# Softmax inverses sent through DRAM instead of through a transpose on TensorE, in a hybrid attention layer on one core

## The chip, the cores and the metric

The kernel runs on one core of a Trainium2 chip. The metric is the device time of one execution in microseconds (us). The core has five engines with a queue each: TensorE (PE; its weight loads are shown apart as PEld), VectorE (DVE), ScalarE (ACT), GpSimd (POOL) and SyncE (SP), which here only issues transfers. The queues run side by side; each runs its instructions in the order in which they are written, and they wait for each other with semaphores.

## The reference, cut to what matters

Two layers (DEPTH = 2), 1024 tokens, width 1024, float32. In each layer one projection of the normed input gives the queries, keys and values of two attention branches and two sets of gate logits:

```
h = rms_norm(x);  qa, ka, va, qb, kb, vb, gate_logits = split(h @ w_in)
A (8 heads of 64, bias table, 576-key band per 64-token chunk):
    p = softmax(q k^T / 8 + bias);                 y_a = (p v) @ w_branch_a
B (8 heads, 2 key heads, rotary, 128-key window, one learned sink per head):
    m = max(max(s), sink);  p = exp(s - m) / (sum exp(s - m) + exp(sink - m)); y_b = (p v) @ w_branch_b
x = x + (g_a * y_a + g_b * y_b) @ w_out;   x = x + SwiGLU(rms_norm(x))
```

The kernel does not divide p by its sum before the product with v. It multiplies the 64 output features of a head by 1 / sum afterwards, per token. The output is stored with features on the partitions and tokens along the row, while the sums stand with tokens on the partitions; so the inverses have to be turned, and each repeated over the 64 partitions of its head.

## The kernel before, in words

Each layer has four stretches: the input projection, attention, the branch and output projections, and the feed-forward part. Only attention is touched; in the trace its scores run from 281 to 527 us in layer 0 and from 1613 to 1860 us in layer 1.

Attention runs over UNITS = 128 **units**. A unit is one head of one 128-query block in branch A, or one chunk of 64 tokens (two heads of it side by side) in branch B. Units go by groups (GROUPS = 4) of 32: a phase of 16 A units (PHASE = 16), then a phase of 16 B units. Two units that follow each other (e = 0 and 1) make one pair, and a pair has one output tile of 128x128. Every engine has its own loop over **slots** `s`, written out by hand; there is no scheduler. In slot s:

- PE (`attention`, L1501 to 1527) computes the scores of unit s (L1412, L1413), one step of the gate projection (`gate_step`; three 512-column matmuls, L1266, L1270, L1271), turns the softmax rows of unit s-2 (`turn`, L1424), and in even slots turns the inverses of unit pair s-5 (`turn_wide`, L1464), multiplies the pair s-3 with the values (`weigh`, L1452), and takes the other gate steps. At some slots it turns a part of v (`turn_values`, L1387). `turn_wide` writes in the same PSUM bank as `turn_values`: so it waits for ACT's copies of the values (`v_ready`), and `turn_values` waits for `head_scaled`.
- DVE takes the maximum of the scores plus bias (`row_max`, L2691), and in odd slots multiplies a pair's outputs by the turned inverses (`scale_heads`, L2719), in even slots computes the inverses of a pair (`invert_pair`, L2708 and L2710; L2697 for the sinks). The rest is splitting queries, keys and rotary operands (L2639, L2648, L2651, L2662 to 2671) and the gate logits (L2732).
- ACT copies a pair's outputs from PSUM to `x_sb` (`take_heads`, L1857), copies the turned rows (`take_turned`, L1846) and the values (`take_values`, L1815), and takes the exponential with the row sum (`soften`, L1825; L1829 for the sinks).
- POOL repeats each pair of inverses over 64 columns (`repeat_inverse`, L1246, into `wide`), and between these splits the weight tiles of the gate projection in high and low halves (`split_part`, L1228, L1231).
- SP loads q, k, v parts (L988, L993, L950), bias rows (L1113), rotary tables (L1094) and weight tiles (L896), and saves gate logits (L1003); it issues one after the other, each after its own waits.

The gate steps are filler work for PE. How many stand in a slot is a table, `fill_rate` (L229): `FILL_A` for A phases (one row for group 0, one for the others), `FILL_B` steps spread evenly over the B phases.

After the last unit PE has the last gate tile to do (`last_gates`, L1482), while ACT and DVE split the scaled outputs (`split_o`, L1882) for the branch projections.

## Time and profile before

| | |
|---|---|
| median of 3 runs | 2699.23 us (2695.42 to 2701.89) |
| profiled execution | 2699.5 us, of which the span from first to last instruction 2697.5 us |
| TensorE granted clock, mean | 0.994 |
| PE busy | 2633.4 us (98%) |
| DVE busy | 1919.6 us (71%) |
| ACT busy | 1155.7 us (43%) |
| POOL busy | 296.0 us (11%) |

PE is the busiest engine over the whole span, but its share counts a matmul up to its modelled end; inside attention there are gaps. A row of the timeline or of the waits names the idle time before an instruction and what ended it ("<-DVE stat L2691"). PE and PEld are two rows of one engine: a wait can be booked on the weight load (PEld), while a former matmul still runs on PE.

### The profile page before, as it was taken

Reading aid. Unit: us, or ns where it says so; the run is one execution under the profiler, and the core shown is the slowest. Engines: PE = TensorE matmul, PEld = TensorE weight load, DVE = VectorE, ACT = ScalarE, POOL = GpSimd, SP = SyncE. Lnnn points to the kernel's source line nnn. Section 1 sums busy time; section 2 is a strip of 40 time slices with the busy share of each in tenths; the row PEclk is TensorE's granted clock in tenths of the full one; section 3 lists DMA queues with packets and bytes.
Section 4 is the critical chain, followed back from the end, with each engine's and each line's share of the span. In section 5 each row is a group of like instructions: output and inputs, shape, how many; then the busy total and the mean of one; then the engine's idle time right before and its main releaser. Section 6 shows DMA issues by size and latency. Waiting matters only on the chain. (4 is left out here: it accounts for less than half of the span.)

```text
span 2697.5 us, 36792 instructions
## 1 busy us (share of the span) xinstructions
PE 2633.4 (98%) x12920; PEld 2146.6 (80%) x12920; DVE 1919.6 (71%) x3579; ACT 1155.7 (43%) x2365; POOL 296.0 (11%) x518
## 2 busy tenths in 40 slices
PE   8999999999999999999999999999999999999998
PEld 6888767788888888888878886677888888888887
DVE  8766666654787777768996666666447887776687
ACT  6222677632533333344542227776325333333444
POOL 0000212244200000000000012223440000000000
PEclk9999999999999999999999999999999999999999
DMA  4323433253223332386423243332531322334843
GB/s 150 121 102 118 149 98 103 73 174 123 94 94 106 113 108 88 109 266 177 151 102 117 105 147 110 111 96 80 194 125 50 127 98 92 107 114 128 269 127 125
DMA packets 185397, 333.22 MB, mean 124 GB/s; under 512 B 17280, under 2 KB 62976, under 8 KB 185216
## 3 DMA queue, kind: packets, MB, share of 16 engines
q1 hardware_dynamic: 176992, 307.67, 34.7%
q10 hardware_dynamic: 8224, 23.20, 2.5%
q8 instruction: 105, 1.72, 0.3%
q14 instruction: 76, 0.62, 0.1%
HBM read 237.09 MB, written 92.80 MB: 122 GB/s over the span
## 5 line engine op out<-in xcount | busy, mean ns | idle before, releaser
L1278 PE MATMUL ps<-op_hi,up_hi 128*128 128x512 f32 x1232 | 479.9, 390 | 2.5 <-DVE third_sum L2871 2.5
L1280 PE MATMUL ps<-op_hi,up_lo 128*128 128x512 f32 x1232 | 479.3, 389 | 0.0
L1279 PE MATMUL ps<-op_lo,up_hi 128*128 128x512 f32 x1232 | 479.3, 389 | 0.0
L1278 PE MATMUL ps<-in_hi,up_hi 128*128 128x512 f32 x728 | 286.6, 394 | 2.4 <-DVE up_lo L2367 2.1
L1280 PE MATMUL ps<-in_hi,up_lo 128*128 128x512 f32 x728 | 285.2, 392 | 0.0
L1279 PE MATMUL ps<-in_lo,up_hi 128*128 128x512 f32 x728 | 285.2, 392 | 0.0
L1966 ACT ACTIVATE up_hi<-up_raw 128x512 fp32r<-128x512 f32 x252 | 158.0, 630 | 278.6 <-PE ps L1280 271.4
L1278 PEld LDWEIGHTS ps<-op_hi,up_hi 128*128 128x128 f32 x1232 | 231.2, 188 | 51.2 <-issue 3.3
L1280 PEld LDWEIGHTS ps<-op_hi,up_lo 128*128 128x128 f32 x1232 | 231.2, 188 | 48.1
L1279 PEld LDWEIGHTS ps<-op_lo,up_hi 128*128 128x128 f32 x1232 | 231.2, 188 | 47.9
L1278 PE MATMUL ps<-act_hi,dn_hi 128*128 128x512 f32 x616 | 240.3, 390 | 1.2 <-DVE dn_lo L3046 1.2
L1279 PE MATMUL ps<-act_lo,dn_hi 128*128 128x512 f32 x616 | 239.7, 389 | 0.0
L1280 PE MATMUL ps<-act_hi,dn_lo 128*128 128x512 f32 x616 | 239.6, 389 | 0.0
L1228 POOL CAST w_hi<-w_raw 128x256 fp32r<-128x256 f32 x192 | 83.2, 474 | 1370.1 <-DMA w_raw<-w_lin 1190.0
L1676 ACT ACTIVATE up_hi<-w_quarter 128x512 fp32r<-128x512 f32 x156 | 96.7, 628 | 193.1 <-PE ps L1280 180.4
L2838 DVE TENSOR_TENSOR up_lo<-up_raw,up_hi 128x512 fp32r<-128x512 f32 x252 | 172.4, 686 | 0.0
L1993 ACT ACTIVATE act_hi<-act_raw 128x512 fp32r<-128x512 f32 x154 | 97.0, 630 | 173.8 <-DMA act_raw<-ff_saved 170.9
L1231 POOL TENSOR_TENSOR w_lo<-w_raw,w_hi 128x256 fp32r<-128x256 f32 x192 | 164.4, 885 | 0.0
L1278 PEld LDWEIGHTS ps<-in_hi,up_hi 128*128 128x128 f32 x728 | 138.1, 190 | 32.3 <-DVE up_lo L2367 3.2
L3044 DVE TENSOR_TENSOR act_lo<-act_raw,act_hi 128x512 fp32r<-128x512 f32 x154 | 106.2, 689 | 80.0 <-ACT act_hi L1993 79.6
L1279 PEld LDWEIGHTS ps<-in_lo,up_hi 128*128 128x128 f32 x728 | 137.9, 189 | 28.6
L1280 PEld LDWEIGHTS ps<-in_hi,up_lo 128*128 128x128 f32 x728 | 137.8, 189 | 28.6
(266 smaller groups left out, 5270.0 us busy)
## 6 DMA issues: line engine op xcount, KB each, us to landing
up_raw<-w_gu SPq DMA_DIRECT2D x42, 1024.0 KB, 5.1
act_raw<-ff_saved SPq DMA_DIRECT2D x154, 256.0 KB, 2.7
w_quarter<-w_lin SPq DMA_DIRECT2D x52, 512.0 KB, 4.5
w_raw<-w_lin SPq DMA_DIRECT2D x48, 512.0 KB, 3.6
ff_saved<-ff_block SPq DMA_DIRECT2D x88, 256.0 KB, 2.0
ff_saved<-ff_mix SPq DMA_DIRECT2D x66, 256.0 KB, 2.1
gated<-gates_saved SPq DMA_DIRECT2D x32, 512.0 KB, 4.2
stage<-in_saved SPq DMA_DIRECT2D x48, 256.0 KB, 2.8
```

Source lines behind the costliest of these rows:

```text
L1228: pool.tensor_copy(w_hi[slot][:, k, :], w_raw[raw][:, k, :]).then_inc(hi_made, 1)
L1231: op = pool.tensor_tensor(w_lo[slot][:, k, :], w_raw[raw][:, k, :], w_hi[slot][:, k, :], ALU.subtract)
L1278: pe.matmul(out, w1, x1, start=first, stop=False, skip_group_check=True)
L1279: pe.matmul(out, w1, x0, start=False, stop=False, skip_group_check=True)
L1280: return pe.matmul(out, w0, x1, start=False, stop=last, skip_group_check=True)
L1676: act.activation(up_hi[s % PRODUCTS][:, :, :], in_weight(q, i), ACT.Copy).then_inc(in_raised, 1)
L1966: act.activation(up_hi[s % PRODUCTS][:, :, :], up_src(q, i), ACT.Copy).then_inc(up_raised, 1)
L1993: act.activation(act_hi[r][:, :], act_raw[r][:, :], ACT.Copy).then_inc(act_raised, 1)
L2838: dve.tensor_tensor(up_lo[s % PRODUCTS][:, :, :], up_src(q, i), up_hi[s % PRODUCTS][:, :, :], ALU.subtract).then_inc(up_split, 1)
L3044: dve.tensor_tensor(act_lo[r][:, :], act_raw[r][:, :], act_hi[r][:, :], ALU.subtract)
```

## The change: what it does

- The outputs of a pair are copied from PSUM to `x_sb` by DVE (`take_heads`) one slot earlier in its order than the scaling was, in ACT's place; ACT's copy is gone.
- Maxima, sums, sink terms and inverses stand in four arrays of 16 columns. The inverses of four units (a **quarter**, QUARTER = 4) are computed by one reciprocal of 128x4; the sink terms likewise.
- SP stores the 128x4 inverses turned to a DRAM buffer of 4x128 (`save_inverse`: 512 runs of 4 bytes) and loads them back, each row repeated over 64 partitions, with two transfers into `inverse_rows` (`spread_inverse`). DVE scales four units by one multiply of 128x256 (`scale_heads`). In a quarter that begins at unit 4q the inverse is made at DVE's slot 4q+4 (A) or 4q+5 (B), saved in SP's slot 4q+6, spread in its slot 4q+8, and used in DVE's slot 4q+11.
- `turn_wide` on PE and `repeat_inverse` on POOL are gone, with the two waits that the shared bank asked for. POOL splits the weight tiles as soon as they can be, not in portions by slot.
- The gate steps: `FILL_A`'s second row begins with a step, `FILL_B` rounds up instead of down, and in the first slot of each phase a gate step stands ahead of the scores.
- After attention ACT waits for the last save before its first `o_hi`, and for the last scaling only before `o_hi` 6.

```diff
-NSTAT = 8
+NSTAT = 16
+QUARTER = 4
-FILL_A = ((3, 3, 3, 3, 2, 3, 1, 2, 1, 1, 0, 1, 1, 1, 0, 1), (0, 1, 0, 2, 0, 1, 0, 1, 0, 1, 0, 1, 0, 1, 0, 0))
+FILL_A = ((3, 3, 3, 3, 2, 3, 1, 2, 1, 1, 0, 1, 1, 1, 0, 1), (1, 1, 0, 1, 0, 1, 0, 1, 0, 1, 0, 1, 0, 1, 0, 0))
...
-    return FILL_B[g] * (r + 1) // PHASE - FILL_B[g] * r // PHASE
+    return (FILL_B[g] * (r + 1) + PHASE - 1) // PHASE - (FILL_B[g] * r + PHASE - 1) // PHASE
...
+SAVED_AT, SPREAD_AT, SCALED_AT = 6, 8, 11
...
+            def save_inverse(L, quarter):
+                n = L * QUARTERS + quarter
+                sp.wait_ge(inverse_ready, n + 1)
+                sp.dma_start(inverse_dram[n].rearrange("u n -> n u"), inverse[:, stats_of(quarter)],
+                             allow_slow_non_contiguous=True).then_inc(inverse_saved, 16)
+            def spread_inverse(L, quarter):
+                n = L * QUARTERS + quarter
+                sp.wait_ge(inverse_saved, 16 * (n + 1))
+                if n > 0:
+                    sp.wait_ge(head_scaled, n)
+                for e in range(2):
+                    src = inverse_dram[n].rearrange("(p e) n -> e p n", e=2)[e:e + 1].to_broadcast([HD, 2, P])
+                    sp.dma_start(inverse_rows[e * HD:(e + 1) * HD, :].rearrange("d (p n) -> d p n", p=2), src).then_inc(inverse_spread, 16)
...
-                for s in range(UNITS + 3):
+                for s in range(UNITS + SPREAD_AT):
+                    if s >= SAVED_AT and (s - SAVED_AT) % QUARTER == 0 and s - SAVED_AT < UNITS:
+                        save_inverse(L, (s - SAVED_AT) // QUARTER)
+                    if s >= SPREAD_AT and (s - SPREAD_AT) % QUARTER == 0:
+                        spread_inverse(L, (s - SPREAD_AT) // QUARTER)
...
-                for s in range(UNITS + 2):
-                    if s >= 3 and s % 2 == 1:
-                        repeat_inverse(L, s - 2)
-                    for t, part in split_parts(s):
-                        split_part(L, t, part)
-                for t in range(GATE_TILES, TILES):
+                for t in range(TILES):
                     split(L, t)
...
-                for s in range(UNITS + 5):
+                for s in range(UNITS + 3):
+                    steps = fill_steps(s)
+                    if s % PHASE == 0 and s > 0:
+                        for i, k in steps[:1]:
+                            gate_step(L, i, k)
...
-                    if s >= 6 and s % 2 == 0:
-                        turn_wide(L, s, s - 5)
...
-                        if s >= 6:
-                            pe.wait_ge(head_scaled, L * HEAD_PAIRS + (s - 4) // 2)
                         turn_values(L, c, part)
...
-                    if s >= 5 and s % 2 == 1:
-                        take_heads(L, s - 4)
...
+            def invert(L, quarter):
+                cols = stats_of(quarter)
+                total = row_sum[:, cols]
+                dve.wait_ge(softened, L * UNITS + QUARTER * (quarter + 1))
...
+                dve.reciprocal(inverse[:, cols], total).then_inc(inverse_ready, 1)
+            def take_heads(L, u):
...
+                dve.wait_ge(head_done, n + 1)
+                src = o_ps(u) if mixer == "A" else o_ps(u).rearrange("p (h n) -> p h n", h=2)
+                dve.tensor_copy(x_of(u), src).then_inc(head_free, 1)
+            def scale_heads(L, quarter):
...
+                dve.wait_ge(head_free, L * HEAD_PAIRS + 2 * quarter + 2)
+                dve.wait_ge(inverse_spread, 32 * (n + 1))
+                if mixer == "A":
+                    x = x_sb[:, g, p * P:(p + 2) * P]
+                    dve.tensor_tensor(x, x, inverse_rows[:, :], ALU.mult).then_inc(head_scaled, 1)
```

PE's queue where branch B of group 1 begins (unit 48). `ka_hi` and `kb_hi` are the keys of A and B (scores), `probs` the softmax rows being turned, `wide` the repeated inverses, `va` the values, `w_hi` a gate weight tile. Before:

```order
L1413 MATMUL ps<-ka_lo_94,qs_88 128x384
L1424 MATMUL ps<-ident,probs_107 128x128 x5
L1412 MATMUL ps<-kb_hi_95,qb_first 128x128
L1413 MATMUL ps<-kb_lo_97,qb_first 128x128
L1424 MATMUL ps<-ident,probs_108 128x128 x5
L1464 MATMUL ps<-ident,wide 128x128
L1452 MATMUL ps<-probs_t_112,va 64x128
```

And in the changed kernel, at the same place:

```order
L1419 MATMUL ps<-ka_lo_94,qs_88 128x384
L1430 MATMUL ps<-ident,probs_107 128x128 x5
L1272 MATMUL ps<-in_hi_52,w_hi_230 128x512
L1276 MATMUL ps<-in_lo_59,w_hi_230 128x512
L1277 MATMUL ps<-in_hi_52,w_lo_232 128x512
L1418 MATMUL ps<-kb_hi_95,qb_first 128x128
L1419 MATMUL ps<-kb_lo_97,qb_first 128x128
L1430 MATMUL ps<-ident,probs_108 128x128 x5
L1458 MATMUL ps<-probs_t_112,va 64x128
```

The three matmuls of a gate step stand between the last A rows and the first B scores, and the turn of `wide` ahead of the product with the values is gone.

DVE's queue in the same B phase. The first instruction of each pair on `probs` is `row_max`; `ka_lo` is a key half of the next A phase. Before:

```order
L2691 ISA probs_107,stat<-ps,b_zeros,less_sinks 128x128
L2691 ISA stat 128x1
L2708 TENSOR_TENSOR stat<-stat 128x2
L2710 RECIPROCAL stat<-stat 128x2
L2691 ISA probs_108,stat<-ps,b_zeros,less_sinks 128x128
L2691 ISA stat 128x1
L2697 TENSOR_TENSOR stat<-sink_rows,stat 128x2
L2719 TENSOR_TENSOR x_sb<-ps,x_sb 128x2x64
```

And in the changed kernel, over one quarter:

```order
L2717 COPY x_sb<-ps 128x2x64
L2703 TENSOR_TENSOR sink_term<-row_sum,sink_term 128x4
L2705 RECIPROCAL inverse<-sink_term 128x4
L2744 TENSOR_TENSOR logit_118<-ps,rstd 128x512
L2682 ISA probs_108,neg_max<-ps,b_zeros,less_sinks 128x128
L2682 ISA neg_max 128x1
L2682 ISA probs_109,neg_max<-ps,b_zeros,less_sinks 128x128
L2682 ISA neg_max 128x1
L2717 COPY x_sb<-ps 128x2x64
L2731 TENSOR_TENSOR x_sb<-x_sb,inverse_rows 128x2x128
```

Four small instructions per pair became four per quarter, each pair has a copy, and every second pair also the scaling multiply, which waits for a transfer and has the next `row_max` behind it.

SP's queue from the last loads of group 1's B phase into the A phase behind it (`stage` and `swapped` take operands, `w_raw` the gate weight tile). Before:

```order
L988 DMA stage_103<-in_saved 64x512 x2
L896 DMA w_raw_225<-w_lin 128x1024
L993 DMA stage_104<-in_saved 128x512
L993 DMA stage_103<-in_saved 128x512
L950 DMA swapped<-in_saved 32x512 x4
```

And in the changed kernel:

```order
L903 DMA w_raw_228<-w_lin 128x1024
L1118 DMA inverses_saved<-inverse 128x4x1
L995 DMA stage_103<-in_saved 64x512 x2
L1129 DMA inverse_rows<-inverses_saved 64x2x128 x2
L1000 DMA stage_104<-in_saved 128x512
L1118 DMA inverses_saved<-inverse 128x4x1
L1000 DMA stage_103<-in_saved 128x512
L957 DMA swapped<-in_saved 32x512 x4
```

Between the loads of the operands there is now, per quarter, one save and two spreads, and the spread stops SP until the save has landed.

## Rows read from the trace of the kernel before

**Rows 1.** The page: busy time by engine.
```profile
PE 2633.4 (98%) x12920; PEld 2146.6 (80%) x12920; DVE 1919.6 (71%) x3579; ACT 1155.7 (43%) x2365; POOL 296.0 (11%) x518
```

**Rows 2.** Busy time of stretches: start:end, length, PE PEld DVE ACT POOL, PEclk.
```profile
280.00:532.00 252.00, 234.08 (x1660) 177.51 (x1659) 158.67 (x547) 176.22 (x527) 58.21 (x124) 0.99 0.32 99
337.00:344.00 7.00, 6.43 (x31) 4.54 (x31) 3.41 (x15) 5.66 (x17) 0.59 (x2) 0.76 0.31 81
```

**Rows 3.** PE's and PEld's waits, 280 to 532 us: total, times, longest.
```profile
PE ps L1464 <- ACT vb L1815: 3.8, 4, 2.0
PE ps L1464 <- ACT va L1815: 2.9, 5, 1.4
PE ps L1412 <- DVE qb_second L2648: 1.5, 1, 1.5
PE ps L1464 <- POOL wide L1246: 1.2, 1, 1.2
...
PEld ps L1464 <- issue: 14.0, 22, 2.4
...
PEld ps L1387 <- DVE x_sb L2719: 5.0, 15, 0.6
```

**Rows 4.** Timeline of PE at 305 and 306 us: start, length, instruction.
```profile
305.27 0.27 PE L1424 MATMUL ps<-ident,probs 128*128 128x128 f32 x1
...
306.55 0.71 PE L1424 MATMUL ps<-ident,probs 128*128 128x128 f32 x5
```

**Rows 5.** Timeline of PE in the last B phase, layer 1.
```profile
1851.45 0.44 PE L1452 MATMUL ps<-probs_t,vb 128*64 128x128 f32 x4
...
1852.09 0.45 PE L1266 MATMUL ps<-in_hi,w_hi 128*128 128x512 f32 x1
...
1852.84 0.38 PE L1424 MATMUL ps<-ident,probs 128*128 128x128 f32 x2
...
1853.30 0.30 PE L1464 MATMUL ps<-ident,wide 128*128 128x128 f32 x1
1853.69 0.44 PE L1452 MATMUL ps<-probs_t,vb_odd 128*64 128x128 f32 x4
...
1856.43 0.44 PE L1452 MATMUL ps<-probs_t,vb 128*64 128x128 f32 x4
```

**Rows 6.** Groups of instructions, 280 to 532 us: busy, mean ns, idle before.
```profile
L2719 DVE TENSOR_TENSOR x_sb<-ps,x_sb 128x128 f32<-128x128 f32 x64 | 18.4, 288 | 1.0 <-PE ps L1464 1.0
L2710 DVE RECIPROCAL stat<-stat 128x2 f32<-128x2 f32 x64 | 10.6, 166 | 1.5 <-DVE stat L2708 0.2
L2732 DVE TENSOR_TENSOR logit<-ps,rstd 128x512 f32<-128x512 f32 x14 | 9.6, 688 | 0.1
```

**Rows 7.** Waits of DVE, 280 to 532 us.
```profile
DVE probs L2691 <- PE ps L1413: 53.3, 63, 2.2
...
DVE stat L2708 <- ACT stat L1829: 6.1, 16, 1.0
```

**Rows 8.** Transfers, 280 to 532 us: KB each, median us from issue to landing.
```profile
gates_saved<-logit SPq DMA_DIRECT2D x14, 256.0 KB, 2.1
...
swapped<-in_saved SPq DMA_DIRECT2D x28, 64.0 KB, 2.3
```

**Rows 9.** The same view of the whole execution.
```profile
sinks<-sink_in SPq DMA_DIRECT2D x1, 8.0 KB, 9.7
```

**Rows 10.** SP's own timeline: start, time in which it issues.
```profile
376.51 0.34 SPq L993 DMA_DIRECT2D stage<-in_saved  x1
378.95 0.58 SPq L1094 DMA_DIRECT2D rope<-rope_in  x1
...
397.45 1.09 SPq L988 DMA_DIRECT2D stage<-in_saved  x2
```

**Rows 11.** Timeline at the end of attention in layer 0.
```profile
527.79 0.38 ACT L1846 ACTIVATE probs_t<-ps 128x256 f32<-128x256 f32 x1
...
529.18 0.44 PE L1452 MATMUL ps<-probs_t,vb 128*64 128x128 f32 x4
```

More of the change, by code:

```diff
@@ L585, in x_of, with stat_of, stats_of @@
             return x_sb[:, tile:tile + 2, chunk * CHUNK:(chunk + 1) * CHUNK]
+        def stat_of(u):
+            return slice(u % NSTAT, u % NSTAT + 1)
+        def stats_of(quarter):
+            first = QUARTER * quarter % NSTAT
+            return slice(first, first + QUARTER)
         def turned_to(u):
@@ L1228, in split_part @@
                     pool.tensor_copy(w_hi[slot][:, k, :], w_raw[raw][:, k, :]).then_inc(hi_made, 1)
-                else:
-                    pool.wait_ge(hi_made, W_PARTS * number + first + 1)
+                for part in range(W_PARTS):
+                    k = slice(part * KT // W_PARTS, (part + 1) * KT // W_PARTS)
+                    pool.wait_ge(hi_made, W_PARTS * number + part + 1)
                     op = pool.tensor_tensor(w_lo[slot][:, k, :], w_raw[raw][:, k, :], w_hi[slot][:, k, :], ALU.subtract)
-                    if first == W_PARTS - 1:
-                        op.then_inc(tile_ready, 1)
@@ L1870, in attention @@
                         soften(L, s)
+                    if s >= QUARTER and s % QUARTER == 0 and unit(s - 1)[0] == "B":
+                        soften_sinks(L, s // QUARTER - 1)
                     for e in range(2):
@@ L2712, in scale_heads, with add_sinks @@
-            def scale_heads(L, u):
+                                         ALU.add, ALU.min, neg_max[:, stat_of(u)]).then_inc(scores_free, 1)
+            def add_sinks(L, quarter):
+                _, g, _, _ = unit(QUARTER * quarter)
+                cols = stats_of(quarter)
+                both = sink_rows[:, :].rearrange("p (a h) -> p h a", h=2)[:, g // 2:g // 2 + 1, 2 * L:2 * L + 2]
+                dve.wait_ge(scores_free, L * UNITS + QUARTER * (quarter + 1) + 1)
+                dve.tensor_tensor(sink_term[:, cols].rearrange("p (c e) -> p c e", e=2), both.to_broadcast([P, 2, 2]),
+                                  neg_max[:, cols].rearrange("p (c e) -> p c e", e=2), ALU.add).then_inc(sink_step, 1)
@@ new lines, in scale_heads @@
+            def scale_heads(L, quarter):
+                mixer, g, _, p = unit(QUARTER * quarter)
+                n = L * QUARTERS + quarter
+                dve.wait_ge(head_free, L * HEAD_PAIRS + 2 * quarter + 2)
[3 more added lines that the diff above has]
+                    dve.tensor_tensor(x, x, inverse_rows[:, :], ALU.mult).then_inc(head_scaled, 1)
+                else:
+                    tile, chunk = GROUPS + g // 2 * 2, chunk_of(g, p)
+                    x = x_sb[:, tile:tile + 2, chunk * CHUNK:(chunk + 2) * CHUNK].rearrange("p h (c n) -> p h c n", c=2)
+                    dve.tensor_tensor(x, x, inverse_rows[:, :].rearrange("p (c h n) -> p h c n", c=2, h=2), ALU.mult).then_inc(head_scaled, 1)
@@ L2734, in attention @@
             def attention(L):
-                for s in range(UNITS + 6):
+                for s in range(UNITS + SCALED_AT):
                     if s < UNITS:
                         row_max(L, s)
-                    if s % 2 == 1 and s >= 7:
-                        scale_heads(L, s - 6)
-                    if s % 2 == 0 and 1 <= s <= UNITS:
-                        invert_pair(L, s - 1)
+                    if s % 2 == 1 and 5 <= s < UNITS + 4:
+                        take_heads(L, s - 4)
+                    for late in range(2):
+                        quarter, first = divmod(s - QUARTER - late, QUARTER)
+                        if first == 0 and 0 <= quarter < QUARTERS:
+                            sunken = unit(QUARTER * quarter)[0] == "B"
+                            if late == 0 and sunken:
+                                add_sinks(L, quarter)
+                            if late == (1 if sunken else 0):
+                                invert(L, quarter)
+                    if s >= SCALED_AT and (s - SCALED_AT) % QUARTER == 0:
+                        scale_heads(L, (s - SCALED_AT) // QUARTER)
                     for e in range(2):
```

138 lines of the change are left out of this document (51 added, 87 removed).

## The prediction

> **What bounds the kernel now.** The page comes first: PE is busy for 2633.4 of 2697.5 us [rows 1], so a change can only pay where PE has work less or stands still. Then the stretches: the attention part of layer 0, 280 to 532 us, has 234.1 us of PE busy in 252.0, DVE 158.7 and ACT 176.2 [rows 2]; layer 1 repeats it. So some 18 us per layer are open idle time, and more is hidden, since a matmul counts up to its modelled end. The waits of that stretch tell where: PE's row for the turn of `wide` (L1464) waits 3.8 + 2.9 us for ACT's copies of the values and 1.2 us for POOL, and its weight load stands for 14.0 us more with no releaser named; the transposes of the values wait 5.0 us for DVE's scaling [rows 3]. Last the waits of DVE: it waits 53.3 us for PE's scores [rows 7]. So in attention no single engine is full. PE, DVE and ACT hand units round in a ring, PE has the least slack, and its largest stops are at the very instruction that the change removes.
>
> **What the change removes from PE.** 64 transposes per layer (one per output pair, as many as L2719 has [rows 6]), 128 in all. Five transposes in a row take 0.71 us, one 0.27 [rows 4]: (0.71 - 0.27) / 4 = 0.11 us for each further one, 128 x 0.11 = 14.1 us. Not every one is on the path. At 1853 us the turn of `wide` starts 0.39 us before the product with the values, more than the transpose takes: the product waits for ACT's copy in any case [rows 5]. That is so in roughly a quarter of the pairs, so I take 0.75 x 14.1 = 10.6 us; ends 0 and 14.1.
>
> **The waits at the turn of `wide`.** Booked on PE: 3.8 + 2.9 + 1.2 = 7.9 us per layer; with the weight load's 14.0 it is 21.9, but a wait booked there runs partly beside an older matmul [rows 3]. For two layers the ends are 15.8 and 43.8 us; I take 24, nearer the row in which PE itself is idle. With the instruction the wait goes, and next to be late are the copies of the turned rows (`probs_t`) and the maxima. ACT's queue is in the same order as before, minus one copy per pair, so PE runs ahead of it by a step, and then meets it. I let 60% stay as gain: 14.4 us; ends 0 and 24. The wait at the end of attention (POOL, 1.2 us) is among them: the last product starts 1.39 us after ACT began the last copy of 0.38 us [rows 11], and the changed queue has nothing between.
>
> **The waits at the turns of the values.** They waited for `head_scaled`, 5.0 us per layer on the weight load [rows 3], 10 in all, partly beside older work: 6 as the size, 60% of it stays, 3.6 us; ends 0 and 10.
>
> **The gate step ahead of a phase.** It costs nothing in sum, since the number of steps is the same, and it fills a hole: at unit 48 PE waits 1.5 us for `qb_second` [rows 3]. From the first matmul of a step to what follows it are 1852.84 - 1852.09 = 0.75 us [rows 5]. One such hole per layer, 2 x 0.7 = 1.4 us; ends 0 and 3.0. The new fill table moves steps by a slot or less; I cost it at nothing, since a step hides the copy of `probs_t` wherever it stands between turn and product, and the skipped ones now fall into odd slots, ahead of a turn instead of behind it.
>
> **The clock.** Between 337 and 344 us the granted clock is 0.76 of full speed, so a part of that stretch runs at 1.2 instead of 2.4 GHz; before it PE had stood for 2.0 us, the longest of the waits for ACT's `vb` copy [rows 2, 3]. 7.0 x 0.24 = 1.7 us per layer; if the wait shrinks the fall may go. I take 2 us for both layers; ends 0 and 3.4.
>
> **What it moves to DVE.** Removed per layer: 64 multiplies of 0.288, 64 reciprocals of 0.166 and 64 sink additions that I price like a reciprocal: 18.4 + 10.6 + 10.6 = 39.6 us. Added: 64 copies from PSUM, for which the trace has no row; the multiply of the same size from PSUM takes 0.288, the reciprocal of two columns 0.166, these are my ends and I take 0.288: 18.4. Further 32 multiplies of 256 columns: 128 columns take 0.288, 512 take 0.688 [rows 6], so 0.288 + 128 x (0.688 - 0.288) / 384 = 0.42, 13.4 us; 32 reciprocals and 32 sink additions, 10.6. Together 42.4, or 2.8 us more of 158.7: no new bound by itself. But order matters: in every second odd slot the copy and the multiply, 0.71 us instead of 0.29, now stand ahead of the next maximum. If all of that were on the path it would be 64 x 0.42 = 27 us; DVE waits 53.3 us per layer for scores [rows 7], so most of it is covered: 3 us. The wait of DVE for ACT's sink exponentials, 6.1 us per layer [rows 7], goes since the sum is now read a slot later; on PE's path I credit 1 us for both layers, ends 0 and 12.
>
> **What it adds on SP, and the wait behind it.** The multiply waits for `inverse_spread`, and behind it on DVE stands the next `row_max`, for which PE waits. In a B phase there are six slots from the reciprocal to the multiply. Four slots take 1856.43 - 1851.45 = 4.98 us in the last group, which has 12 gate steps in 16 slots [rows 5]; that is 1.25 each, in the other groups (14 steps) 0.75 x 2 / 16 = 0.09 more, 1.34. Without the transpose (0.11 per two slots) they are 1.19 and 1.28, six of them 7.1 and 7.7, less 0.33 for sum and reciprocal: 6.8 and 7.4 us. Against that stands the chain. A store of 128 runs lands in 2.1 us [rows 8]. SP issues 128 runs in 0.34 us and 256 in 0.58 [rows 10], so 512 in 1.06, 0.72 more: 2.8 us, and I take 3.2 for the writes of 4 bytes; ends 2.1 and 9.7, the latter the slowest small transfer of the trace, queued behind large ones [rows 9]. Then two spreads: the second is issued 0.55 us after the first (half of 1.09 [rows 10]) and lands 2.3 us later, as a 64 KB load does [rows 8]: 2.85. In sum 6.1, with semaphores 6.2: inside 6.8 and 7.4, though narrowly. SP itself is held 3.2 + 1.1 = 4.3 us of a quarter of 4.8 to 5.1, and the operand loads between (1.09 us for two) can make it late by half a microsecond. I take 0.5 us in 8 of the 32 B quarters: 4 us; low end 0, high end below. In A phases a unit has up to five times as many columns and there are seven slots, so nothing is late.
>
> The Trainium skill ("DMA: Bandwidth & Descriptors", section Specifications) says that transfers with runs below 512 bytes make the DMA engine read, modify and write. The trace of before has no store with runs that short, so no run here shows it; it is a reason for the third rival below, and if it made the save cost twice my value it would be that case.
>
> **The sum.** Gains 10.6 + 14.4 + 3.6 + 1.4 + 2 + 1 = 33.0, losses 3 + 4 = 7, net 26 us. The profiled execution took 2699.5 us, within 0.3 us of the median of the runs (2699.23), so the forecast is 2673.5, rounded 2673 us.
>
> **Rivals.**
> - *The waits only move.* PE meets ACT and DVE a step later and waits there. For it: ACT and DVE already sit at 70% and 63% of the stretch [rows 2], and ACT's late copies of the values come from ACT's own backlog. Against it: DVE waits longer for PE than PE for DVE. Then remain the transposes, a fifth of the 24 us and the clock, 10.6 + 4.8 + 2 - 7 = 10: 2689 us.
> - *DVE's heavier slots are on the path.* The 27 us are paid instead of 3: 33 - 27 - 4 = 2, so 2698 us. Against it speak the same 53.3 us.
> - *The save is slow, and B phases run at the pace of the transfers* (slower than before). Each quarter's multiply then waits, the next maximum with it, and six slots last as long as the chain. With a save of x us a slot is (x + 2.95 + 0.33) / 6, against a mean of 1.26; over 128 B slots it eats all gains of 30 us from an excess of 0.24 on, a slot of 1.50, x = 5.7 us. At x = 6.5 it is 1.63, 0.37 x 128 = 47 us lost, 33 - 47: about 2714 us. At the end of 9.7 us it would be 2.16 per slot, 115 us lost, some 2780. For it: 512 runs of 4 bytes, and SP standing still behind them. Against it: all stores of the stretch land in about 2 us.
>
> **Chances.** Forecast 0.50, waits that move 0.22, DVE on the path 0.13, slow save 0.15. The likeliest case alone reaches from 2658 (most of the waits gone) to 2684. For the whole I give 2655 to 2703: 0.06 lies below, 0.13 above, almost all of it the slow save. A difference of 0.2% (5.4 us) is about what a measurement of this kernel can tell from none. Faster by more: 0.49 of the first case, 0.19 of the second, 0.04 of the third, 0.01 of the last, 0.73. Within: 0.01 + 0.02 + 0.06 + 0.01 = 0.10. Slower: the rest, 0.01 + 0.03 + 0.13 = 0.17.
>
> **What would show it.** Right: no idle above 0.5 us before the product with the values in group 0 of A, the stretch from the first score to the first matmul of the last gate tile shorter by about 13 us in each layer, and nothing changed behind it, since PE's last gate tile covers the later start of `o_hi`. The save's row should have 2.8 to 3.6 us to landing, the spread's 2.3 to 2.6, and DVE's multiply little idle time before it. Wrong: a row in which that multiply waits for the transfer in most B quarters, with PE's B scores waiting for the maxima behind it (slow save); PE waits for `probs_t` or the maxima grown by what L1464 has lost (moved waits); or ACT waiting for `stage` loads that SP issued late, a case which I hold small, since a half-microsecond of lateness is less than the room between a load and its use.

## The result, and the profile after

The changed kernel takes 2980.5 us (median of 4 runs, 2968.41 to 2982.84), against 2697.32 us (4 runs) for the kernel before on the same chip: ratio 1.1038, 95% interval 1.1004 to 1.1072. It is 283 us slower, where 26 us faster was forecast. The profiled execution has a span of 2980.9 us and a mean granted clock of 0.938, against 0.994.

The page, then the stretch of attention in layer 0, cut at 656 us, 5 us after its last scores (before at 532; the scores ended at 525); the third line is the B phase of group 1 (columns as in [rows 2]):

```profile
PE 2695.8 (90%) x12792; PEld 2182.7 (73%) x12792; DVE 1914.1 (64%) x3515; ACT 1127.9 (38%) x2205; POOL 244.9 (8%) x390
```

```profile
280.00:656.00 376.00, 258.83 (x1581) 192.71 (x1579) 154.67 (x503) 160.18 (x442) 31.64 (x55) 0.77 0.41 73
...
422.30:474.10 51.80, 30.44 (x167) 21.85 (x168) 14.59 (x61) 14.61 (x49) 4.20 (x8) 0.70 0.36 53
```

PE, 98% busy in [rows 1], is at 90%. The stretch is 376 us long instead of 252 [rows 2]. PE's busy time in it rose from 234 to 259 us for less work: the granted clock fell from 0.99 to 0.77, so close to half of the stretch ran at 1.2 instead of 2.4 GHz, each time after PE had stood (2.0 to 5.3 us in one piece). The other 99 of the 124 us are idle time. Layer 1 lost as much: from its first to its last scores there are 372.4 us, before 243.9. DVE, ACT and POOL do less than before and became no bound.

The waits of PE, DVE, ACT and SP in that stretch, as in [rows 3, 7]:

```profile
PE ps L1458 <- ACT probs_t L1844: 39.6, 8, 9.2
PE ps L1418 <- DVE neg_max L2682: 28.8, 13, 6.1
PE ps L1393 <- DMA stage<-in_saved: 18.0, 4, 9.0
```

```profile
DVE probs L2682 <- PE ps L1419: 51.6, 38, 10.0
...
DVE x_sb L2727 <- DMA inverse_rows<-inverses_saved: 33.2, 8, 8.6
DVE ka_lo L2631 <- ACT ka_hi L1776: 30.9, 11, 7.4
DVE x_sb L2731 <- DMA inverse_rows<-inverses_saved: 24.8, 8, 7.2
```

```profile
ACT ka_hi L1776 <- DMA stage<-in_saved: 63.8, 10, 11.6
...
ACT qs L1774 <- DMA stage<-in_saved: 17.2, 4, 8.3
```

```profile
SPq L1129 <- DMA inverses_saved<-inverse: 170.4, 30, 9.1
SPq L1126 <- DVE x_sb L2727: 31.8, 12, 6.0
```

Two kinds of late data stand here side by side. DVE waits 58 us for the spread inverses (L2727 is the multiply of an A quarter, L2731 of a B quarter). But ACT waits 81 us for `stage`, a load of q or k that has nothing to do with the inverses, and DVE's `ka_lo` waits for ACT behind it. Before, ACT's wait for `stage` was 0.3 us:

```profile
ACT ka_hi L1780 <- DMA stage<-in_saved: 0.3, 1, 0.3
```

The transfers say the same. `stage` before (280 to 532 us), then three rows of now [rows 8]:

```profile
stage<-in_saved SPq DMA_DIRECT2D x21, 256.0 KB, 2.8
```

```profile
stage<-in_saved SPq DMA_DIRECT2D x21, 256.0 KB, 8.6
inverse_rows<-inverses_saved SPq DMA_DIRECT2D x60, 64.0 KB, 3.6
...
gates_saved<-logit SPq DMA_DIRECT2D x13, 256.0 KB, 9.4
```

The store of the gate logits landed in 2.1 us and now takes 9.4. One quarter shows the chain, in the timelines of SP, DVE, ACT and PE:

```profile
333.20 0.46 SPq L1118 DMA_DIRECT2D inverses_saved<-inverse  x1
333.79 2.41 SPq L1137 DMA_DIRECT2D rel_sb<-rel  x4
343.52 1.26 SPq L1129 DMA_DIRECT2D inverse_rows<-inverses_saved  x2
344.88 2.11 SPq L995 DMA_DIRECT2D stage<-in_saved  x2
```

```profile
348.13 0.42 DVE L2727 TENSOR_TENSOR x_sb<-x_sb,inverse_rows 128x256 f32<-128x256 f32 x1 [7.12 <-DMA inverse_rows<-inverses_saved]
```

```profile
349.04 0.63 ACT L1776 ACTIVATE ka_hi<-stage 128x512 fp32r<-128x512 f32 x1 [8.57 <-DMA stage<-in_saved]
...
350.87 0.36 ACT L1844 ACTIVATE probs_t<-ps 128x256 f32<-128x256 f32 x1
```

```profile
351.33 0.69 PE L1458 MATMUL ps<-probs_t,vb_odd 128*64 128x128 f32 x4 [9.79 <-issue]
```

From the save's issue to the spread's issue pass 10.3 us; over all 64 quarters it is 7.6 to 12.0, median 9.4. SP issues the four `rel_sb` loads in it and then stands, from 336.2 to 343.5 us, so the `stage` loads behind it are issued only at 344.88. DVE's multiply waits 7.1 us with the maxima behind it. But what ends last ahead of PE is on ACT: it stands 8.6 us for `stage`, and the copy of the turned rows (`probs_t`) that PE's product reads stands behind that. PE's row names no releaser; its 9.8 us end 0.1 us after that copy. So in this quarter SP's standing reached PE by the late load; the multiply had been done since 348.55.

### The profile page after: what moved, and what is told of

It is laid out like the page before. It is cut to its first block and busy times, and to the rows that moved or that the text cites. A ratio compares the mean times of both kernels' runs of the same rounds, so it can differ in the third digit from the quotient of the medians.

```text
span 2980.9 us, 36091 instructions
## 1 busy us (share of the span) xinstructions
PE 2695.8 (90%) x12792; PEld 2182.7 (73%) x12792; DVE 1914.1 (64%) x3515; ACT 1127.9 (38%) x2205; POOL 244.9 (8%) x390
## 5 line engine op out<-in xcount | busy, mean ns | idle before, releaser
L1820 ACT ACTIVATE probs<-probs,neg_max 128x128 f32<-128x128 f32 (+5 forms) x256 | 138.7, 542 | 96.6 <-DVE neg_max L2682 95.1
```

What stands on the lines that cost most here:

```text
L1820: act.activation(buf[:, c0:c1], buf[:, c0:c1], ACT.Exp, bias=neg_max[:, stat_of(u)], scale=-1.0, accum_out=row_sum[:, stat_of(u)]).then_in ...
```

## The experiments

**First set: the whole loss, and where it sits.** Its expectations number the theories; 1 is that the transfers of the inverses are the whole loss.

`no_transfer` leaves out save and spreads; DVE multiplies by a constant.

```diff
-                        save_inverse(L, (s - SAVED_AT) // QUARTER)
-                        spread_inverse(L, (s - SPREAD_AT) // QUARTER)
+                        pass
...
+            pool.memset(inverse_rows[:, :], 0.01).then_inc(consts_made, 1)
```

> The changed kernel without save and spreads: SP issues neither, DVE multiplies by a constant buffer instead of the inverses, and nothing waits for a transfer (the output is therefore not scaled by the true inverses). All the rest of the change stays: DVE's copies, the multiply of 128x256 per four units, no turn of wide on PE, the moved gate steps. Theory 1 (the transfers are the whole loss, whether by the wait of DVE or by what they do to other transfers): 2660 to 2685 us, the 2673 us of the forecast less its 4 us for the spread. Theory 2 (DVE's heavier odd slots, the copy and the multiply ahead of the next maximum, carry a part of the loss): above 2700 us, up to 2900.

Measured: 2660.9 us, ratio to before 0.9862 (0.9846 to 0.9878). The transfers are the whole loss; all the rest of the change gains 37.5 us. From the first to the last scores of a layer there are 226.3 us, against 244.1 before (they end near 525 us, not 527 as the text ahead of the prediction has it) and 370.7 in the changed kernel. The stretch from 281 to 513 us, columns as in [rows 2]:

```profile
281.00:513.00 232.00, 218.75 (x1596) 166.76 (x1595) 157.41 (x514) 161.00 (x446) 34.40 (x60) 1.00 0.35 106
```

Almost the same matmuls (1596 against 1581 recorded) keep PE busy for 219 us here and for 259 in the changed kernel. So of the loss some 40 us per layer, 80 of 320 us, are busy time that goes with the lower clock; the rest is time in which PE stands.

`late_use` keeps the 4-byte saves, but spreads and uses the inverses much later:

```diff
-SAVED_AT, SPREAD_AT, SCALED_AT = 6, 8, 11
+SAVED_AT, SPREAD_AT, SCALED_AT = 6, 16, 19
```

> The changed kernel with the spread at SP slot 4q+16 instead of 4q+8 and the multiply at DVE slot 4q+19 instead of 4q+11: ten slots between save and spread, so that nobody stands still for the save to land. The same transfers are issued. Theory 1a (the loss is the wait: DVE's multiply and SP stand for the chain of save and spread): 2670 to 2700 us. Theory 1b (the save holds the DMA queues, so that the operand loads and gate logits behind it land late, whoever waits for the save itself): still above 2800 us, with landings of 8 us for the operand loads and ACT and DVE waiting for stage.

Measured: 2897.1 us, ratio 1.0733 (1.0703 to 1.0763). Room for the save gives back 83 of 283 us. How much of the loss is the wait for the save can't be read from this alone: SP now stands 103 us between 280 and 680 us for the multiply of the quarter before, more than the 50 us of the changed kernel. `save_only` below shows the part that needs no such wait.

`flat_save` stores the same 2 KB as 128 runs of 16 bytes, a token's four inverses in each:

```diff
-                sp.dma_start(inverse_dram[n].rearrange("u n -> n u"), inverse[:, stats_of(quarter)],
-                             allow_slow_non_contiguous=True).then_inc(inverse_saved, 16)
+                sp.dma_start(inverse_dram[n].rearrange("u (r c) -> (u r) c", c=QUARTER), inverse[:, stats_of(quarter)]).then_inc(inverse_saved, 16)
```

> The changed kernel, where the save writes the inverses as they stand, 128 runs of 16 bytes into one 2 KB block, instead of turned (512 runs of 4 bytes with 512 bytes between neighbours of a partition); the spread then reads the block in another order, so the outputs are scaled by inverses of other tokens. Bytes, waits and places are those of the changed kernel. Theory 1c (the cost is in the number of short runs): the save needs a quarter of its time, 3 to 4 us instead of about 9, and the kernel takes 2680 to 2730 us. Theory 1d (any store to DRAM followed by a load back under a standing SP costs this): 2900 us or more.

Measured: 2689.9 us, ratio 0.9954 (0.9937 to 0.9971). Its transfers between 280 and 520 us:

```profile
stage<-in_saved SPq DMA_DIRECT2D x22, 256.0 KB, 3.5
inverse_rows<-inverses_saved SPq DMA_DIRECT2D x61, 64.0 KB, 2.7
...
gates_saved<-logit SPq DMA_DIRECT2D x13, 256.0 KB, 3.8
...
inverses_saved<-inverse SPq DMA_DIRECT2D x31, 2.0 KB, 3.1
```

The save lands in 3.1 us and the other transfers nearly as before. It is the form of the save that costs. I took the number of its runs for the cause; that fell later.

`gates_only` is the kernel before, with nothing but the new fill table and the gate step ahead of a phase's first scores:

```diff
+                    if s % PHASE == 0 and s > 0:
+                        for i, k in steps[:1]:
+                            gate_step(L, i, k)
...
```

> The kernel before with the gate steps alone changed: the new fill table and the gate step ahead of a phase's first scores. The forecast credited 1.4 us of gain, ends 0 and 3: 2696 to 2698 us. If the skipped steps in odd slots let the copies of probs_t stand bare between turn and product less often, up to 5 us more; if the moved steps take cover away elsewhere, up to 5 us slower.

Measured, in 5 runs: 2688.5 us, ratio 0.9962 (0.995 to 0.9975), a gain of 10 us, more than any reading had. In the profiled runs 1.8 us of it lie ahead of the first scores (279.2 against 281.0 us), where the edit changes nothing, so in that pair of runs it is 8.

**Second set: the save alone, and a save in another form.**

`save_only` is `no_transfer` with the 32 saves of each layer put back on SP; nobody reads them. (The texts on record for `save_only` and `rows_saved` say 16 saves and 16 transposes; it is 32 of each in a layer.) Two completion counters take turns, so SP waits for the save before the last, and DVE for one four quarters back before it overwrites the inverses; between 280 and 680 us no wait ended on either. `save_only_act` has the saves on ACT's own queue.

```diff
+                if n >= 2:
+                    sp.wait_ge(saved_of[n % 2], 16 * ((n - 2) // 2 + 1))
                 sp.wait_ge(inverse_ready, n + 1)
...
```

> The changed kernel without its spreads, but with its 16 saves of the inverses (512 runs of 4 bytes each) issued on SyncE's queue where the changed kernel issues them; VectorE multiplies by a constant and nobody uses what was saved (the scaling of the outputs is left out). SyncE stands only for the save before the last. The kernel without any of these transfers took 2661 us. Theory Q (a save holds up the transfers issued behind it, and engines wait for their late loads): stage loads land in 7 to 9 us in attention instead of 2.8, and the time is 2780 to 2890 us. Rival W (what costs is the chain save, spread, multiply, release of a bank): nothing waits for the save here, so 2655 to 2675 us. The kernel with late users (2897 us) speaks for Q, since spacing the chain gave back only 83 of 283 us.

> As the kernel with saves alone, but ScalarE issues them on its own DMA queue, at the same place in the row of units (scaling left out likewise). If what is held is SyncE's queue (each of its descriptors waits its turn behind the save's), SyncE's loads land in about 3 us again and the time is 2661 to 2690 us. If what is held is the DMA engines or the memory that the save writes to, whatever queue it stands on, stage loads land in 7 to 9 us again and the time is that of the kernel with saves alone within 20 us. I hold the second likelier, 3 to 2, as the spreads of the changed kernel too landed late without standing directly behind a save.

Measured: 2799.9 us on SP (1.0381, 1.0365 to 1.0397) and 2840.7 us on ACT (1.0539, 1.0524 to 1.0553). Transfers between 280 and 520 us, on SP first:

```profile
stage<-in_saved SPq DMA_DIRECT2D x19, 256.0 KB, 8.2
...
gates_saved<-logit SPq DMA_DIRECT2D x11, 256.0 KB, 8.7
```

```profile
stage<-in_saved SPq DMA_DIRECT2D x18, 256.0 KB, 10.8
...
gates_saved<-logit SPq DMA_DIRECT2D x10, 256.0 KB, 9.7
...
inverses_saved<-inverse ACTq DMA_DIRECT2D x21, 2.0 KB
```

A save that nobody waits for costs 139 us: ACT waits 42.4 us for `stage` before `ka_hi` (280 to 680 us), before 0.3. And SP's loads are late too when the save stands on another queue: what is held up is not SP's queue but something behind both, the DMA engines or the memory. The dearer case was the one on ACT, by 41 us, outside the 20 us that I had allowed; why, no run tells.

`rows_saved` turns the inverses on the chip: one transpose of PE per quarter, in the spare half of the output bank, a copy by DVE, and a save of 4 runs of 512 bytes.

```diff
-SAVED_AT, SPREAD_AT, SCALED_AT = 6, 8, 11
+SAVED_AT, SPREAD_AT, SCALED_AT = 8, 11, 15
...
-                sp.dma_start(inverse_dram[n].rearrange("u n -> n u"), inverse[:, stats_of(quarter)],
-                             allow_slow_non_contiguous=True).then_inc(inverse_saved, 16)
+                sp.dma_start(inverse_dram[n], inverse_turned[:, :]).then_inc(inverse_saved, 16)
...
+                    pe.transpose(turned_ps(u), inverse[:, stats_of(quarter)], ident[:, :])
...
+                    dve.tensor_copy(inverse_turned[:, :], turned_ps(u))
```

> The changed kernel with the inverses turned on the chip first: TensorE transposes the quarter's 128x4 inverses once for four units (16 transposes in all), VectorE copies the 4x128 result, and SyncE saves 4 runs of 512 bytes instead of 512 runs of 4; the save is issued in slot 8 of a quarter instead of 6, the spread in 11, the first use in 15. By theory Q the save then lands in 2 to 3 us, stage loads in about 3 us, and the time is near that of the kernel without the transfers (2661 us) plus 16 copies of about 0.3 us and some waiting: 2662 to 2682 us. If the spreads (two of 128 partitions each) are a cost of their own, 2685 to 2700 us, as the kernel with a flat save (2690 us) would then have shown for the same reason.

Measured: 2691.5 us (11 runs), ratio 0.9981 (0.9973 to 0.999). The loads land in about 3 us, but the time missed its 2662 to 2682. It falls in the range of the other reading, a cost of the spreads themselves; the third set shows another reason.

`flat_late` is the flat save with slots 6, 10, 15, and the spread ahead of the save where both fall in one slot:

> The kernel with the flat save (128 runs of 16 bytes; the outputs are scaled by other tokens' inverses), with the spread issued in slot 10 and ahead of the next save, and the first use in slot 15, so that SyncE and VectorE hardly wait for a transfer. The flat save took 2690 us, 29 us over the kernel without transfers. If those 29 us are the waits of SyncE and VectorE for save and spread: 2664 to 2678 us. If they are other loads held for a while by the 16-byte runs: 2682 to 2692 us, no change.

Measured: 2785.8 us, ratio 1.0331 (1.0317 to 1.0346), 96 us worse than `flat_save`, which neither reading had. SP between 280 and 680 us:

```profile
SPq L1125 <- DVE x_sb L2730: 71.6, 15, 9.1
SPq L1125 <- DVE x_sb L2726: 69.2, 13, 8.7
```

There is one buffer `inverse_rows`. With 10 and 15 the spread of a quarter (slot 4q+10) stands in SP's order ahead of the slot in which DVE makes the multiply of the quarter before (4q+11), and SP waits 141 us for it, with every load behind it (57 us in `flat_save`). The room between spread and use must stay under four slots.

**Third set: the slots.** The three kernels with rows saved differ in one line each, and `late_gap` is `late_use` with 6, 14, 16:

```diff
-SAVED_AT, SPREAD_AT, SCALED_AT = 8, 11, 15
+SAVED_AT, SPREAD_AT, SCALED_AT = 8, 11, 14
```

> As the kernel with the inverses turned on TensorE and saved as rows (2691.5 us), with save, spread and first use in slots 8, 11, 14 instead of 8, 11, 15. There is one buffer for the spread inverses, so the spread of a quarter waits for the multiply of the quarter before, which comes 4 slots before this quarter's own. With 8, 11, 15 both fall in one slot, and SyncE stood 94 us at that wait between 280 and 680 us, with the loads behind it. Now one slot lies between them. If this standing is what the 30 us over the kernel without transfers are: 2672 to 2684 us. If they are the added transposes, copies and issues (32 of each): 2688 to 2694 us.

> As rows_a with 8, 12, 15: the same one slot between the multiply before and the spread, but the save has 4 slots to land before SyncE waits for it. It lands in 2 to 3 us, and two slots of a B phase are 3 us, so the fourth slot should give nothing: within 4 us of rows_a. Should it be over 5 us faster, SyncE stood for the save, not for the multiply.

> As rows_a with 8, 12, 14: two slots between the multiply before and the spread, and two from the spread to its use. SyncE's standing for the multiply should be nearly gone, but VectorE has 3 us in a B phase for a transfer of 2.6 us behind 1.2 us of issues, and may now wait for it, 1 us in each of 16 B quarters. If SyncE's standing decides: 2665 to 2680 us, faster than rows_a by 3 or more; if VectorE's wait decides: slower than rows_a.

> The kernel with 4-byte saves and late users, with save, spread and use in slots 6, 14, 16 instead of 6, 16, 19. The version with 6, 16, 19 took 2897 us, 97 us more than the saves alone without any spread (2800 us), and SyncE stood 103 us between 280 and 680 us for the multiply of the quarter before. Theory S (beside the held transfers, worth 139 us, the rest is SyncE standing at its waits with the loads behind it): two slots of room instead of one take a third to two thirds of the standing away, 2830 to 2870 us. Rival: the rest is what the spreads' own transfers lose behind a save; then it stays at 2885 to 2905 us, or becomes slower, as the users wait 2 slots after the spread instead of 3.

| kernel | slots | us | ratio to before (95%) |
|---|---|---|---|
| rows_a | 8, 11, 14 | 2668.2 | 0.9887 (0.9872 to 0.9902) |
| rows_b | 8, 12, 15 | 2677.9 | 0.9923 (0.9908 to 0.9938) |
| rows_c | 8, 12, 14 | 2682.0 | 0.9937 (0.9923 to 0.9952) |
| late_gap | 6, 14, 16 | 2930.9 | 1.0857 (1.0835 to 1.0879) |

`rows_a` beats both kernels, by 30 us the one before. Nothing of the change is left out in it; it is 7 us over `no_transfer`, with 32 transposes and copies per layer as added work. Its rows, the waits between 280 and 680 us and the groups between 280 and 520:

```profile
SPq L1131 <- DVE x_sb L2741: 35.8, 15, 6.5
SPq L1131 <- DVE x_sb L2745: 21.2, 10, 3.9
```

```profile
L2729 DVE COPY inverse_turned<-ps 4x128 f32<-4x128 f32 x32 | 8.8, 274 | 0.1
L1463 PE MATMUL ps<-ident,inverse 128*4 128x128 f32 x32 | 8.7, 272 | 2.7 <-ACT probs_t L1853 1.5 <-DVE inverse L2714 1.2
```

One slot less between spread and use gave 23 us. `rows_b` missed its forecast (10 us slower than `rows_a`, not within 4), and `rows_c` went the way of its second branch, though DVE waits for the spread only 16.3 us in it, against 7.0 in `rows_a`, so that wait alone doesn't explain its 14 us. A spread in slot 12 stands behind the next quarter's save, which is issued in the same slot and waits for DVE's copy; that order moved SP's standing from the multiply to that copy (63.5 us in `rows_b`, 14.9 in `rows_a`). `late_gap` did not give theory S what it forecast: SP's standing for the multiply fell from 103 to 29 us, and yet the time rose by 34. But it doesn't refute the theory, for its slot 14 has the order of `rows_b`: the spread stands behind a later quarter's save, and at that save SP now stands 122 us for DVE's inverses (21 in `late_use`). SP's standing only changed its place, and DVE's wait for the spread grew:

```profile
SPq L1118 <- DVE inverse L2705: 122.4, 27, 9.8
```

```profile
DVE x_sb L2727 <- DMA inverse_rows<-inverses_saved: 74.6, 15, 9.0
DVE x_sb L2731 <- DMA inverse_rows<-inverses_saved: 61.6, 13, 8.6
```

In `late_use` these two were 28.9 and 25.3. In the slots tried here, with a save of 4-byte runs, moving spread and use changed who waits, not whether.

**Fourth set: what in the save is slow.** All five are `save_only` with its save changed: a quarter of the runs, or all 512 moved apart in DRAM.

```diff
-        inverse_dram = nc.dram_tensor("inverses_saved", (DEPTH * QUARTERS, QUARTER, P), F32, kind="Internal").ap()
+        inverse_dram = nc.dram_tensor("inverses_saved", (DEPTH * QUARTERS, QUARTER, P, 16), F32, kind="Internal").ap()
...
-                sp.dma_start(inverse_dram[n].rearrange("u n -> n u"), inverse[:, stats_of(quarter)],
+                sp.dma_start(inverse_dram[n][:, :, 0].rearrange("u n -> n u"), inverse[:, stats_of(quarter)],
...
```

> The kernel with the saves alone (2800 us, 139 over the kernel without transfers), with a quarter of each save: the inverses of one of the four units, 128 runs of 4 bytes (the scaling is left out). If the price goes by the count of runs: stage loads land in 3.3 to 4.5 us and the time is 2665 to 2695 us, like the 128 runs of 16 bytes. If a 4-byte run costs more than a 16-byte one whatever their number, or a save has a fixed price: over 2720 us.

> The saves alone, 512 runs of 4 bytes as before, but every run is written 64 bytes apart in DRAM instead of right behind its neighbour (the scaling is left out). If the runs are slow because neighbours, written by different DMA engines, fall into one small block of DRAM and wait for each other: stage loads near 3 us, 2661 to 2700 us. If it is the count of small writes: as the saves alone, 2785 to 2815 us. I hold the second likelier, 2 to 1.

> As save_spaced, with the runs 512 bytes apart, for blocks larger than 64 bytes (the scaling is left out). Neighbours waiting for each other: 2661 to 2700 us here, and more at 64 bytes where the block is larger than that. Count of small writes: 2785 to 2815 us, the same as at 64 bytes and as side by side.

> As save_spaced (4-byte runs 64 bytes apart, 2664 us), but 16 bytes apart, so that 4 runs share 64 bytes of DRAM instead of 1, or of 16 side by side (2800 us); the scaling is left out. The flat save, with four 16-byte runs to 64 bytes, landed in 3.1 us. If the price goes by how many writes fall into one block of 64 bytes: 4 of 16, so 139 us x 4/16 = 35 us over 2661: 2680 to 2715 us. If the block in which writes wait for each other is 16 bytes or smaller: 2661 to 2670 us. If only the count mattered, 2800 us, which the spaced saves already speak against.

> The same with the runs 32 bytes apart: 2 share 64 bytes (the scaling is left out). A block of 64 bytes: 139 us x 2/16 = 17 us, so 2665 to 2690 us, between the ones at 16 and at 64 bytes. A block of 32 bytes or smaller: as at 64 bytes, 2661 to 2668 us.

| 4-byte runs of a save | from one to the next | us (2 runs each; save_only and no_transfer 4) | `stage` lands in |
|---|---|---|---|
| 512 (save_only) | 4 bytes | 2799.9 | 8.2 us |
| 128 (save_quarter) | 4 bytes | 2761.8 | 7.6 us |
| 512 | 16 bytes | 2668.0 | 3.4 us |
| 512 | 32 bytes | 2665.4 | 3.0 us |
| 512 | 64 bytes | 2663.8 | 2.7 us |
| 512 | 512 bytes | 2661.5 | 3.0 us |
| none (no_transfer) | | 2660.9 | 2.8 us |

The row that kills my theory of the count is that of the 128 runs of 4 bytes, between 280 and 520 us:

```profile
stage<-in_saved SPq DMA_DIRECT2D x21, 256.0 KB, 7.6
...
inverses_saved<-inverse SPq DMA_DIRECT2D x25, 0.5 KB, 9.3
```

A quarter of the runs lands as late as all of them (9.4 us to the next issue in the changed kernel), and costs 101 of the 139 us. And 512 runs of 4 bytes cost 3 us in the whole kernel once they start 64 bytes apart, which these few runs can't tell from nothing: the ratio to before is 0.9882 (0.9853 to 0.9911), that of `no_transfer` 0.9862 (0.9846 to 0.9878). Size and count are the same there; only the neighbourhood differs. The loss comes from 4-byte writes directly beside each other. The 16-byte runs of `flat_save` also lie side by side, and cost little: four of them fill 64 bytes, as four of the 4-byte runs do at 16 bytes from one to the next. That distance suffices for nearly all of it (8 bytes was not tried), at the edge of what I had expected for a small block (2661 to 2670 us). I had held this the less likely reading, 1 to 2.

**Last, the changed kernel itself with only the addresses changed:**

```diff
-        inverse_dram = nc.dram_tensor("inverses_saved", (DEPTH * QUARTERS, QUARTER, P), F32, kind="Internal").ap()
+        inverse_dram = nc.dram_tensor("inverses_saved", (DEPTH * QUARTERS, QUARTER, P, 16), F32, kind="Internal").ap()
...
-                    src = inverse_dram[n].rearrange("(p e) n -> e p n", e=2)[e:e + 1].to_broadcast([HD, 2, P])
+                    src = rope_in[4 * (n % 8):4 * (n % 8) + 4, 0, 0:P].rearrange("(p e) n -> e p n", e=2)[e:e + 1].to_broadcast([HD, 2, P])
```

> The changed kernel (2980.5 us) with everything in its place, the save of 512 runs of 4 bytes in slot 6, the spread in slot 8, the multiply in slot 11, and all the waits, but with the 4-byte runs written 64 bytes apart. So that the spread still reads rows of 512 bytes, it takes them from an input instead (the outputs are scaled by numbers of the rotary table, not by the inverses). Theory N (neighbouring 4-byte writes in one block are the whole loss): the save lands in 2 to 4 us, stage loads in about 3.5 us, and the time is that of the kernel with the flat save, 2690 us, within 12 us. Rival: with the chain of save, spread and multiply behind it, 512 small writes cost something wherever they go: 2720 us or more.

Measured: 2725.7 us, ratio 1.0103 (1.0086 to 1.012). The edit takes 255 of the 283 us away, with the save, the spreads and all waits in place. But it misses theory N's 2690 us by 36: the rival's bound of 2720 is passed. Its rows between 280 and 680 us, transfers and then DVE:

```profile
stage<-in_saved SPq DMA_DIRECT2D x21, 256.0 KB, 4.4
...
inverse_rows<-rope_in SPq DMA_DIRECT2D x64, 64.0 KB, 4.3
```

```profile
DVE x_sb L2731 <- DMA inverse_rows<-rope_in: 18.7, 7, 7.2
```

In `flat_save` these are 3.5, 2.7 and 7.8 us, and its save lands in 3.1 us against 4.2 here. So 512 separate writes still delay what shares the path where someone waits for them, or the other source of the spread does; the run changed both and can't tell these apart.

## Why the prediction was wrong

- **What bounds the kernel: right.** PE has the least slack: without the transfers it is busy for 219 of 232 us in attention, DVE for 157 and ACT for 161.
- **The gains: near in sum, in part by luck.** Forecast 33.0 less 3 for DVE's order, 30; measured 37.5 without the transfers. On the kernel before, the gate step with its table gave 10 (8 of them in the part that it touches), forecast 1.4 with ends 0 and 3: mis-sized. I had priced one hole at unit 48; the edit also changes the fill table, which I costed at nothing, and which of the two brings it no run tells. If it gives as much in the changed kernel, the remaining 27 us stand against 28.6 forecast for transposes, waits, clock and sinks less DVE's order; how they split was not tried.
- **DVE: its prices were right.** The copy from PSUM takes 286 ns, forecast 288; the reciprocal of four columns 178, forecast 166; the multiply of 256 columns 420 in A as forecast, 476 in B. DVE's wait for scores did not become smaller (51.6 against 53.3) in a stretch half as long again, and in `no_transfer` nothing stands behind DVE that cost the gain.

```profile
L2717 DVE COPY x_sb<-ps 128x128 f32<-128x128 f32 x62 | 17.7, 286 | 0.0
L2727 DVE TENSOR_TENSOR x_sb<-x_sb,inverse_rows 128x256 f32<-128x256 f32 x16 | 6.7, 420 | 33.2 <-DMA inverse_rows<-inverses_saved 33.2
L2731 DVE TENSOR_TENSOR x_sb<-x_sb,inverse_rows 128x256 f32<-128x256 f32 x13 | 6.2, 476 | 24.8 <-DMA inverse_rows<-inverses_saved 24.8
```

- **SP's issue: wrong on the safe side.** 512 runs were to take 1.06 us; the timeline has 0.46 at 333.20 us and 0.59 at 349.60.
- **The save's price: the step that failed.** "I take 3.2 for the writes of 4 bytes; ends 2.1 and 9.7." It is 7.6 to 12.0 us until the spread is issued, near and over the upper end. SP's waits in between end on the save 30 times (170 us) and on DVE's multiply 20 times (46 us), so most of it is the save. The choice went by the nearest rows, stores of 2048-byte runs, when the one property that differed, 4-byte runs side by side, was the one that mattered. The Trainium skill ("DMA: Bandwidth & Descriptors", section Specifications) has runs under 512 bytes read, modified and written. That warned in the right direction, but it goes by size alone, and by it the runs 16 bytes apart (4 bytes each) should cost as much as those side by side: 2668 against 2800 us say that it isn't the size alone.
- **The price of a slow save: the second failure, and the larger one.** At 9.7 us the rival gave "some 2780". The measured 2980 is 200 more, because the rival charged only DVE's wait in 128 B slots. `save_only` shows what it left out: with no one waiting for a save, 139 us go to loads that are late. "In A phases ... nothing is late" fails with it: DVE's multiplies of A quarters wait 33.2 us for the spread, and the A phases of groups 1 and 2 take 49.1 and 50.5 us, against 33.0 and 32.1 before, like the B phases with 51.8 and 38.2 against 25.1 and 25.5 (from first scores to first scores, layer 0). The last case of the text, ACT waiting for `stage`, "which I hold small", is 63.8 us before `ka_hi` in 10 waits, and 17.2 before `qs`. Among ACT's rows only the wait for PE's turned rows is longer (70.4 us in 52 waits). The other 181 us of the 320 over `no_transfer` come with the spreads and the waits for them. They can't be split cleanly, since `late_use` and `late_gap` each turned one wait into another.
- **Behind attention: a term put at nothing.** The text has "nothing changed behind it", since the last gate tile covers the later start of `o_hi`. In the changed kernel the last multiply of layer 0 starts at 679.74 us after a wait of 11.96 for its spread, and PE stands 8.18 us ahead of the branch projections that begin at 681.45. From the last scores of a layer to the first of the next, or to the end, it takes 18 and 13 us more than `no_transfer`, 32 of the 320.
- **The chances.** The slow save had 0.15 and the range ended at 2703. With a price known only between 2.1 and 9.7 us, a deciding point of 5.7 in its middle and SP standing behind it, that was too little: the text itself had 2780 us for the upper end, and the range stopped 77 us short of it.

## What to carry to other kernels

Before a small store to DRAM is put in a loop, look at what lies beside each run: if 4-byte elements from different partitions fall side by side, turn the tile on the chip first, so that the runs are long, or let them start at least 16 bytes apart. Price a transfer in two parts, what its reader waits and what it does to every other transfer of the stretch, and for the second part look at all loads whose slack is shorter than its duration. With one buffer, keep the room between load and use under one period, or the issuing queue stands with everything behind it; and look what stands ahead of the load in its own slot, since a later save there makes it wait too (`rows_b`, `late_gap`).

## What was not expected of the hardware

- 4-byte writes directly beside each other in DRAM: 128 of them land in 9.3 us, and until then 256 KB loads take 7.6 instead of 2.8 us. 16 bytes apart, 512 of them leave those loads at 3.4 us.
- It is not bound to a queue: with the saves on ACT's queue, SP's loads took 10.8 us. What the writes wait for, the runs don't show.
- The lower clock is part of such a loss: PE's busy time in the stretch is 259 us at a granted clock of 0.77, and 219 us at 1.00 in `no_transfer`, with 1581 and 1596 recorded matmuls.
